# Two of the three split-precision products of 256-column activations under one pass of the weights

## The reference, cut to what matters

```python
def mixer_block(h, ...):                      # first block, 2 layers
    u = h @ w_in                              # 1024 x (proj + 4096 gate columns)
    ...
    g = jax.nn.sigmoid(gates.reshape(bsz, seq, N_BRANCH, D_MODEL))
    merged = (g[:, :, 0] * (y_a @ w_up_a) + g[:, :, 1] * (y_b @ w_up_b)
              + g[:, :, 2] * (y_c @ w_up_c) + g[:, :, 3] * (y_d @ w_up_d))
    return merged @ w_out

def swiglu(h, w_in, w_out):                   # w_in 1024 x 5632, w_out 2816 x 1024
    gate, up = jnp.split(h @ w_in, 2, axis=-1)
    return (jax.nn.silu(gate) * up) @ w_out
```

## Time and profile before

| | us |
|---|---|
| median of 3 runs | 2862.05 |
| profiled execution, its own time | 2864.3 |
| span of the profiled execution | 2862.5 |
| TensorE matmul busy | 2715.0 |
| TensorE weight loads busy | 2372.7 |
| VectorE busy | 1645.2 |
| ScalarE busy | 1133.2 |
| mean granted TensorE clock | 0.976 of 2.4 GHz |

### The profile page before, as it was taken

The page is one execution under the profiler, slowest core; times in us unless marked ns, Lnnn a source line. Parts: engine busy times, 40 slices in busy tenths (PEclk is TensorE's granted clock), DMA queues, the critical chain, the costliest instruction groups (busy, mean ns, idle before and its releaser), DMA issues.

```text
span 2862.5 us, 39149 instructions
## 1 busy us (share of the span) xinstructions
PE 2715.0 (95%) x16098; PEld 2372.7 (83%) x16098; DVE 1645.2 (57%) x2699; ACT 1133.2 (40%) x1743; POOL 0.3 (0%) x5
## 2 busy tenths in 40 slices
PE   7999899899989989999899989999989999899898
PEld 6999899899979978888664868888868888778898
DVE  6656777665567765555541555555555444655654
ACT  6464444545544442222232432222232222345443
POOL 0000000000000000000000000000000000000000
PEclk9999999999999989999999999999999999999999
DMA  5443577444347744444411024445434444311554
GB/s 187 170 139 112 169 228 225 158 148 148 111 169 226 224 154 155 148 137 153 143 53 66 30 74 132 141 146 153 149 103 146 141 154 144 128 38 45 177 175 135
DMA packets 114049, 403.22 MB, mean 141 GB/s; under 512 B 12368, under 2 KB 15568, under 8 KB 113744
## 3 DMA queue, kind: packets, MB, share of 16 engines
q1 hardware_dynamic: 113872, 400.72, 43.5%
HBM read 399.63 MB, written 1.05 MB: 140 GB/s over the span
## 4 chain that ended last, share of the span: by engine, by line
PE 91%; DVE 4%; ACT 3%; issue 2%; DMA 1%; SPq 0%; DVEq 0%; ACTq 0%
PE psum L533 26%; PE psum L534 25%; PE psum L535 25%; PE psum L829 2%; PE psum L856 1%; PE psum L956 1%; PE psum L964 1%; ACT whi L1034 1%; ACT L1062 1%; DVE wlo L1411 1%; PE psum L529 0%; PE psum L922 0%; PE psum L890 0%; PE psum L903 0%; PE psum L894 0%
## 5 line engine op out<-in xcount | busy, mean ns | idle before, releaser
L533 PE MATMUL psum<-HHI,whi 128*128 128x256 f32 (+1 forms) x3456 | 1126.4, 326 | 60.1 <-DVE HLO L1477 32.7
L534 PE MATMUL psum<-HLO,whi 128*128 128x256 f32 (+1 forms) x3456 | 1117.0, 323 | 0.0
L535 PE MATMUL psum<-HHI,wlo 128*128 128x256 f32 (+1 forms) x3456 | 1116.0, 323 | 0.0
L1411 DVE TENSOR_TENSOR wlo<-wring,whi 128x1024 fp32r<-128x1024 f32 x590 | 707.6, 1222 | 392.5 <-ACT whi L1034 390.0
L1034 ACT ACTIVATE whi<-wring 128x1024 fp32r<-128x1024 f32 x590 | 607.0, 1054 | 466.6 <-PE psum L535 442.8
L533 PEld LDWEIGHTS psum<-HHI,whi 128*128 128x128 f32 x3456 | 668.8, 194 | 126.6 <-issue 65.9
L534 PEld LDWEIGHTS psum<-HLO,whi 128*128 128x128 f32 x3456 | 669.1, 194 | 49.0 <-issue 1.4
L535 PEld LDWEIGHTS psum<-HHI,wlo 128*128 128x128 f32 x3456 | 668.4, 193 | 47.9
L533 PE MATMUL psum<-HIDHI,whi 128*128 128x256 f32 (+1 forms) x1056 | 357.2, 338 | 0.0
L534 PE MATMUL psum<-HIDLO,whi 128*128 128x256 f32 (+1 forms) x1056 | 357.2, 338 | 0.0
L535 PE MATMUL psum<-HIDHI,wlo 128*128 128x256 f32 (+1 forms) x1056 | 357.2, 338 | 0.0
(11 more groups left out here) (279 smaller groups left out, 2021.1 us busy)
## 6 DMA issues: line engine op xcount, KB each, us to landing
wring<-ffn_in SPq DMA_DIRECT2D x264, 512.0 KB, 4.2
wring<-mod_w SPq DMA_DIRECT2D x144, 512.0 KB, 4.3
wring<-ffn_out SPq DMA_DIRECT2D x96, 448.0 KB, 3.5
wring<-w_proj SPq DMA_DIRECT2D x66, 512.0 KB, 3.4
wring<-w_gate SPq DMA_DIRECT2D x64, 512.0 KB, 3.7
wring<-ffn_out SPq DMA_DIRECT2D x48, 512.0 KB, 4.0
wring<-w_up SPq DMA_DIRECT2D x20, 512.0 KB, 3.3
wring<-w_out SPq DMA_DIRECT2D x16, 512.0 KB, 3.5
```

The lines of the kernel that those rows point to most:

```text
L533: mm(out_, w[0], a[0], start=start, stop=False)
L534: mm(out_, w[0], a[1], start=False, stop=False)
L535: return mm(out_, w[1], a[0], start=False, stop=stop)
L1411: TTN(wlo[:, i, :], wring[:, raw_slot(tag, k), :], whi[:, i, :].bitcast(F32), ALU.subtract).then_inc(sem("weights_lo"), 1)
```

## The change

Where the moving side is 256 tokens wide, high and low activations are laid next to each other (`HPAIR[128, 8, 2, 256]`, `HIDPAIR[128, 22, 2, 256]`). The weights' high part then meets both in one matmul of 512 columns, and the weights' low part meets the high activations in a second one of 256 columns, which is added to the first half of the bank. So the bank ends with two sums, high x high + low x high in columns 0 to 255 and high x low in columns 256 to 511, and whoever reads it has to add them. This is done in `gate`, `wo`, in ffi and ffo of the first block, and in the last feed-forward. `proj`, the attentions and everything of 512 columns stay as they are.

The readers: of a gate lot, ScalarE copies the second half and VectorE adds the first. Of `wo` and `ffo`, VectorE adds both halves to X, one after the other, with a wait between. In `ffn` ScalarE copies up's second half to a new buffer `U1`, VectorE adds up's first half to it, the same for gate in `S`, then ScalarE's Silu works on the sum in SBUF, and VectorE multiplies. The order of these among the weights' high and low parts is changed, as the diff shows. The last feed-forward's norm now writes the packed places too.

```diff
+        HPAIR = sb("HPAIR", [P, KT, 2, SEQ], F32R, at=h_at)
+        HHI1, HLO1 = HPAIR[:, :, 0, :], HPAIR[:, :, 1, :]
...
+        HIDPAIR = sb("HIDPAIR", [P, FT, 2, SEQ], F32R, at=arena_at)
+        HIDHI1, HIDLO1 = HIDPAIR[:, :, 0, :], HIDPAIR[:, :, 1, :]
+        S1, U1 = (carve([("S", 2, SEQ)], 2 * FT * SEQ + a)["S"] for a in (0, 2 * SEQ))
...
         def first(tag):
-            return tag[0] in ("n1", "n2")
+            return tag[0] in ("n1", "n2") or tag == ("b2", 1)
...
+            def mm3_pair(bank, w, pair, start, stop):
+
+
+                mm(bank, w[0], pair, start=start, stop=False)
+                return mm(bank[:, 0:SEQ], w[1], pair[:, 0, :], start=False, stop=stop)
...
                 for k in GATE_LOTS[before]:
-                    dense_lot(f"gate{l}", k, SEQ, h_of(("n1", l)))
+                    dense_lot(f"gate{l}", k, SEQ, (HPAIR,))
...
-                dense(f"wo{l}", SEQ, h_of(("n1", l)), lambda c: done("merged", (l, c)))
+                dense(f"wo{l}", SEQ, (HPAIR,), lambda c: done("merged", (l, c)))
...
                 for j in range(FT):
                     k, slot = 2 * j + 1, j % 2
-                    act.wait_ge(*lot_done(tag_in, k))
-                    A(S_[:, slot, 0:n], bank_of((tag_in, k))[:, 0:n], ACT.Silu).then_inc(*freed((tag_in, k), "silu", (tag, j)))
-                    split_ahead(tag_in, k - 1)
+                    if n == SEQ:
+                        act.wait_ge(*lot_done(tag_in, k - 1))
+                        A(U1[:, slot, :], bank_of((tag_in, k - 1))[:, SEQ:BOTH], ACT.Copy).then_inc(*mark("up_lo", (tag, j)))
+                        split_ahead(tag_in, k - 1)
+                        act.wait_ge(*lot_done(tag_in, k))
+                        A(S_[:, slot, :], bank_of((tag_in, k))[:, SEQ:BOTH], ACT.Copy).then_inc(*mark("gate_lo", (tag, j)))
+                        act.wait_ge(*done("gate_sum", (tag, j)))
+                        A(S_[:, slot, 0:n], S_[:, slot, 0:n], ACT.Silu).then_inc(*mark("silu_done", (tag, j)))
...
                     split_ahead(tag_in, k)
                     act.wait_ge(*done("hid_t", (tag, j)))
                     A(hi[:, j, 0:n], S_[:, slot, 0:n], ACT.Copy).then_inc(*mark("hid_hi", (tag, j)))
...
-                    A(gate_places[k // 2][:, k % 2, :], bank_of((f"gate{l}", k))[:, 0:SEQ], ACT.Copy).then_inc(*freed((f"gate{l}", k), "logits", (l, k)))
+                    A(gate_places[k // 2][:, k % 2, :], bank_of((f"gate{l}", k))[:, SEQ:BOTH], ACT.Copy).then_inc(*mark("logits_lo", (l, k)))
...
                 for k in GATE_LOTS[before] if part is None else [GATE_LOTS[before][part]]:
+                    v.wait_ge(*done("logits_lo", (l, k)))
+                    bank = bank_of((f"gate{l}", k))
+                    place = gate_places[k // 2][:, k % 2, :]
+                    TTN(place, place, bank[:, 0:SEQ], ALU.add).then_inc(*freed((f"gate{l}", k), "logits", (l, k)))
                     if k + SLOTS < 4 * KT:
                         split_ahead(f"gate{l}", k)
...
+            def add_tile(m, bank, key, coef, n, event, l=0, pair=False):
+
+                if pair:
+                    x = X[:, m, 0:SEQ]
+                    a, b = bank[:, SEQ:BOTH], bank[:, 0:SEQ]
+                    if coef is None:
+                        ln(TTN(x, x, a, ALU.add))
+                        TTN(x, x, b, ALU.add).then_inc(*freed(key, "x_ready", event))
+                    else:
+                        c = MODS[:, l, coef * KT + m, 0:1]
+                        ln(STT(x, a, c, x, ALU.mult, ALU.add))
+                        STT(x, b, c, x, ALU.mult, ALU.add).then_inc(*freed(key, "x_ready", event))
+                    return
...
                 for j in range(FT):
                     k, slot, up = 2 * j + 1, j % 2, (tag_in, 2 * j)
-                    v.wait_ge(*done("silu", (tag, j)))
-                    TTN(S_[:, slot, 0:n], S_[:, slot, 0:n], bank_of(up)[:, 0:n], ALU.mult).then_inc(*freed(up, "hid_t", (tag, j)))
-                    split_ahead(tag_in, k - 1)
-                    split_ahead(tag_in, k)
+                    if n == SEQ:
+                        gate = bank_of((tag_in, k))
+                        v.wait_ge(*done("up_lo", (tag, j)))
+                        TTN(U1[:, slot, :], U1[:, slot, :], bank_of(up)[:, 0:SEQ], ALU.add).then_inc(*freed(up, "up_sum", (tag, j)))
+                        split_ahead(tag_in, k - 1)
+                        v.wait_ge(*done("gate_lo", (tag, j)))
+                        TTN(S_[:, slot, :], S_[:, slot, :], gate[:, 0:SEQ], ALU.add).then_inc(*freed((tag_in, k), "gate_sum", (tag, j)))
+                        split_ahead(tag_in, k)
+                        v.wait_ge(*done("silu_done", (tag, j)))
+                        TTN(S_[:, slot, :], S_[:, slot, :], U1[:, slot, :], ALU.mult).then_inc(*mark("hid_t", (tag, j)))
...
                     v.wait_ge(*done("hid_hi", (tag, j)))
                     TTN(lo[:, j, 0:n], S_[:, slot, 0:n], hi[:, j, 0:n].bitcast(F32), ALU.subtract).then_inc(*mark("hidden", (tag, j)))
```

More of the change, by code:

```diff
@@ L356, in first @@
         def first(tag):
-            return tag[0] in ("n1", "n2")
+            return tag[0] in ("n1", "n2") or tag == ("b2", 1)
         def h_of(tag):
-            return (HHI1, HLO1, T1) if first(tag) else (HHI, HLO, T2)
+            return (HHI1, HLO1, T1 if tag[0] != "b2" else T2) if first(tag) else (HHI, HLO, T2)
         def sq_of(tag):
-            return SQ1 if first(tag) else SQA if tag[0] == "b2" else SQ
+            return SQA if tag[0] == "b2" else SQ1 if first(tag) else SQ
         def hid_of(tag):
@@ L546, in open_wide @@
                         w = split_blocks(tag, j, KT, P)
-                        last = mm3(bank_of(key)[:, 0:n], (w[0][:, c, :], w[1][:, c, :]), (h[0][:, c, 0:n], h[1][:, c, 0:n]),
-                                   c == 0, c == KT - 1)
+                        wc = (w[0][:, c, :], w[1][:, c, :])
+                        if len(h) == 1:
+                            last = mm3_pair(bank_of(key), wc, h[0][:, c, :, :], c == 0, c == KT - 1)
+                        else:
+                            last = mm3(bank_of(key)[:, 0:n], wc, (h[0][:, c, 0:n], h[1][:, c, 0:n]), c == 0, c == KT - 1)
                         if c == KT - 1:
@@ L554, in tile3 @@
                 for c in range(KT):
-                    last = mm3(bank[:, 0:n], (w[0][:, c, :], w[1][:, c, :]), (h[0][:, c, 0:n], h[1][:, c, 0:n]), c == 0, c == KT - 1)
+                    wc = (w[0][:, c, :], w[1][:, c, :])
+                    if len(h) == 1:
+                        last = mm3_pair(bank, wc, h[0][:, c, :, :], c == 0, c == KT - 1)
+                    else:
+                        last = mm3(bank[:, 0:n], wc, (h[0][:, c, 0:n], h[1][:, c, 0:n]), c == 0, c == KT - 1)
                 return last
@@ L570, in dense, with operand @@
                     dense_lot(tag, k, n, h)
+            def operand(tag, n):
+                return (HPAIR,) if n == SEQ else h_of(tag)
             def ffn(tag_in, tag_out, tag, n):
-                dense(tag_in, n, h_of(tag), lambda c: done("h_ready", (tag, c)))
+                dense(tag_in, n, operand(tag, n), lambda c: done("h_ready", (tag, c)))
                 hi, lo, _ = hid_of(tag)
@@ L586, in ffn @@
                     for c in range(a, b):
-                        last = mm3(bank[:, 0:n], (w[0][:, c - a, :], w[1][:, c - a, :]), (hi[:, c, 0:n], lo[:, c, 0:n]),
-                                   c == 0, c == FT - 1)
+                        wc = (w[0][:, c - a, :], w[1][:, c - a, :])
+                        if n == SEQ:
+                            last = mm3_pair(bank, wc, HIDPAIR[:, c, :, :], c == 0, c == FT - 1)
+                        else:
+                            last = mm3(bank[:, 0:n], wc, (hi[:, c, 0:n], lo[:, c, 0:n]), c == 0, c == FT - 1)
                     lot_event(last, tag_out, k)
@@ L1068, in ffn @@
                     k, slot = 2 * j + 1, j % 2
-                    act.wait_ge(*lot_done(tag_in, k))
-                    A(S_[:, slot, 0:n], bank_of((tag_in, k))[:, 0:n], ACT.Silu).then_inc(*freed((tag_in, k), "silu", (tag, j)))
-                    split_ahead(tag_in, k - 1)
+                    if n == SEQ:
[6 more added lines that the diff above has]
+                        A(S_[:, slot, 0:n], S_[:, slot, 0:n], ACT.Silu).then_inc(*mark("silu_done", (tag, j)))
+                    else:
+                        act.wait_ge(*lot_done(tag_in, k))
+                        A(S_[:, slot, 0:n], bank_of((tag_in, k))[:, 0:n], ACT.Silu).then_inc(*freed((tag_in, k), "silu", (tag, j)))
+                        split_ahead(tag_in, k - 1)
                     split_ahead(tag_in, k)
```

18 lines of the change are left out of this document (10 added, 8 removed).

## The result

| | before | after |
|---|---|---|
| median of 4 runs each, us | 2862.46 (2861.99 to 2864.13) | 2964.14 (2962.53 to 2966.06) |
| span of the profiled execution | 2862.5 | 2962.1 |
| mean granted TensorE clock | 0.976 | 0.969 |

The ratio is 1.0355 [1.0341, 1.0368]: 3.5% slower. The forecast was 2951 in a range of 2925 to 2990. Between the two profiled executions the span grew by 99.6 us where the sum said 88.5.

A forecast was written before the change was run, and what follows sets the result against it. TensorE bounded the kernel before; after the change a ScalarE-VectorE hand-over chain would bound ffi. Chain +93.7, gate -2.3, wo -1.7, ffo -1.6 and last add +0.4 gave +88.5 on 2862.05: 2951 us, range 2925 to 2990.

The forecast's parts named there:

- the sum: Whole program: 93.7 - 2.3 - 1.7 - 1.6 + 0.4 = +88.5 us, added to a median of 2862.05.
- The chain: In ffi, ScalarE and VectorE hand-overs become the bound, 6.28 us a tile against TensorE's 5.53; +93.7 us, chance 0.85.
- The walk: One ffi tile followed through both queues from up copy to next up copy: 6.28 us, 8.57 with a modulation lot.
- the modulation lots: In ffi, each adds 2.29 us to a tile, 10 times in ffi0 and ffi1; three of 1.15 in the last.
- The small terms: Outside ffi: gate net -2.3 us, wo -1.7, ffo -1.6, the very last add to X +0.4.
- The paired step: On TensorE, 512 plus 256 columns replace three matmuls: 345.8 against 358.8 ns, 13.0 ns less a step.
- the 3.0 ns forecast: In ffo, a paired step takes 349.5 ns against 352.5, saving 3.0 ns over 528 steps.
- a dip in ffi: In ffi, a clock fall after a TensorE wait costs 1.7 us, fitting into 3.8 idle us of two tiles.
- The mixers' wait: In the gates, adds behind four low parts lengthen TensorE's wait, about 2.2 us per layer.
- TensorE as the bound: Rival: in ffi both other engines keep busy and TensorE still sets the pace, 2843 us; chance 0.08.
- Loads as the bound: Rival: weight loads set TensorE's pace, so a step falls to its columns' 320 ns, 2776 us; chance 0.02.
- Half clock throughout ffi: Rival: chain idling drops TensorE to 1.2 GHz throughout ffi, 10.2 us a tile, 3160 us; chance 0.05.

The follow-up runs named there:

- experiments on the order: Changed kernel with ffi's copies and sums moved ahead of high and low parts, product ahead of later low part and modulation lot: both 2851.28 us, singly 2877.39 and 2874.05.
- the kernel without the adds: Changed kernel with gate lots still paired, but ScalarE copying only the first half and VectorE's gate add left out: 2957.37 us, ratio 1.0334.
- another order: Changed kernel with both copies and sums first and product earlier in ffi: 2851.28 us; the same with gate and wo back at three matmuls: 2847.06 us.
- either half of the new order alone: Changed kernel with, in ffi, only the product moved ahead of the later low part and modulation lot: 2874.05 us; only both copies and sums first: 2877.39 us.
- The kernel with the better order: Changed kernel, same instructions, in ffi both copies and sums first and product ahead of the later low part and modulation lot: 2851.28 us, ratio 0.9963.
- another kernel: Changed kernel with only ffi's product moved ahead of the later low part and modulation lot, gates unchanged: 2874.05 us, ratio 1.0040.

## Why the prediction was right, and by how much it was off

**The chain was right in place and size.** Forecast were 161.6 us from the first up copy to the last HIDLO in layer 0 and 142.2 in the last feed-forward. The ends in the changed kernel:

```profile
345.14 0.39 ACT L1091 ACTIVATE arena<-psum 128x256 f32<-128x256 f32 x1 [5.73 <-PE psum L542]
...
506.18 0.43 DVE L1842 TENSOR_TENSOR HIDPAIR<-arena,HIDPAIR 128x256 fp32r<-128x256 f32 x1 [0.48 <-ACT HIDPAIR L1103]
...
2747.51 0.39 ACT L1091 ACTIVATE arena<-psum 128x256 f32<-128x256 f32 x1 [5.86 <-PE psum L542]
...
2889.31 0.43 DVE L1842 TENSOR_TENSOR HIDPAIR<-arena,HIDPAIR 128x256 fp32r<-128x256 f32 x1 [0.48 <-ACT HIDPAIR L1103]
```

506.61 - 345.14 = 161.5 and 2889.74 - 2747.51 = 142.2. The walk gave 6.28 and 8.57 us a tile; measured are 6.25 and 8.54. The walk worked because it followed both queues instruction by instruction and took the start of the next instruction, not the end of one, as what a piece costs. The experiments on the order show that this chain, and not the amount of work on any engine, is the cause. That the modulation lots add in full is shown too. The small terms beside it did worse, and nearly all their errors went one way, towards too low a time.

**The 11.1 us that the sum missed** lie outside it: 3.1 and 4.0 in the mixers, 5.3 in the three feed-forwards (1.8, 1.7 and 1.8), less 1.3 in stages that the change doesn't touch. The other 2 us between the forecast and the median come from the profiled execution of before, which took 2.2 us more than its median; that of after took what its median is (2963.89 us).

*The paired step was mis-sized.* The intervals were got by dividing stretches by counts, and the counts include matmuls cut by the edges; from start to start the same stretches of before have 120.0 and 226.7 ns in ffi, 118.3 and 233.3 in ffo. So a step of three was 360.0 ns, and the sum for a pair is 346.7, which leaves the saving at the forecast 13. In wo of layer 0 of the changed kernel, with no wait, the first matmul of a pair starts every 353 ns:

```profile
310.19 0.40 PE L541 MATMUL psum<-HPAIR,whi 128*128 128x512 f32 x1
...
310.54 0.40 PE L541 MATMUL psum<-HPAIR,whi 128*128 128x512 f32 x1
...
311.25 0.40 PE L541 MATMUL psum<-HPAIR,whi 128*128 128x512 f32 x1
```

So 7 ns are saved there, not 13.0. Over the whole mixers, gate and wo together, a step took 350.5 ns on average in layer 0 and 352.2 in layer 1, where it took 359.7 before: 9.2 and 7.5 saved. Over the 640 steps that is 3.0 us less than the sum has. In ffi it didn't matter, as TensorE waits there. In ffo a step went from 355.0 to 353 ns, so the 3.0 ns forecast became 2 or less, some 0.6 us over the 528 steps.

*The clock at the start of ffo was not priced.* The prediction saw that TensorE's idle time could bring the clock down, and argued that a dip in ffi is hidden. In ffi it is: the granted share of the stretch is 0.96 and the chain took its forecast time. But the last one falls where nothing hides it, after the wait for the last HIDLO:

```profile
506.76 0.52 PE L541 MATMUL psum<-HIDPAIR,whi 128*128 128x512 f32 x1 [3.53 <-DVE HIDPAIR L1842]
```

The next 3.5 us have a granted share of 0.56, near 1.2 GHz (the second stretch of the windows above), and that costs 3.5 x 0.44 = 1.5 us. The same stretch at the start of the other two ffo has 0.54 and 0.55. Three feed-forwards make 4.6 of the 5.3, and ffo's steps the rest. This was read from the traces, not tried by itself.

*The mixers' wait was priced, the clock behind it was not.* The 2.2 us for each layer stood for a later wait of TensorE. That one grew by 1.4, and two others by 0.5 to 0.7 together (at 158 us from 0.97 to 1.24, at 195 us from 0.40 to 0.81 in layer 0 and 0.60 in layer 1), so the price was about right, 0.5 too much in two layers. The fall of the clock behind it was missed, some 1.5 a layer in the profile taken. That gives 3.0 + 3.0 - 0.5 = 5.5 of the mixers' 7.1; the rest isn't found, and it is within the 2.4 us by which mixers of the same code differ from profile to profile. That the pairing alone does save there is shown by the step's 359.7 to 350.5 ns, and supported by the whole program: the kernel without the adds takes 2957.37 us, the one with three matmuls in gate and wo 2961.39.

**The rivals.** TensorE as the bound (2843) needed a chain under 5.53 us a tile, which the changed order doesn't give; with another order it came true at 2851 and 2847, so the mechanism was real and the order on the two queues decides it; either half of the new order alone gave back some 80% of the first feed-forward's loss. Loads as the bound are excluded by the same kernel (345 to 347 ns a step, not 320). Half clock throughout ffi: the granted share there is 0.96.

## What to carry to other kernels

Before an engine is relieved by splitting its result over two readers, walk one period of both readers' queues: two in-order engines that hand work to each other several times a period can set a pace that neither one's busy share shows (67% and 46% here). Put each piece that the other engine waits for ahead of pieces that only have to be ready later; here that order alone was worth 4%. Fewer, wider matmuls save only the surplus of each one that goes, here 2 to 13 ns, so this pays in stages of hundreds of steps whose readers have time in hand.

## What the runs showed of the hardware that was not expected

The paired step of 512 and 256 columns has two paces at full clock, with the same code and TensorE never waiting. The kernel with the better order, in ffi0:

```profile
399.94 0.39 PE L541 MATMUL psum<-HPAIR,whi 128*128 128x512 f32 x1
...
400.29 0.39 PE L541 MATMUL psum<-HPAIR,whi 128*128 128x512 f32 x1
...
400.98 0.39 PE L541 MATMUL psum<-HPAIR,whi 128*128 128x512 f32 x1
```

Here it is 347 ns (1.04 us for three steps), in the mixer of the changed kernel above 353 (1.06). Over whole stretches the two values stand apart clearly: the 22 tiles of this ffi run at 346.7 ns a step, which is the sum of the two intervals of before, and most ffo stages at 353.3. Within a stage one pace held until TensorE's next wait; after a wait it could be the other. From ffi to ffo it changed without a wait too, in this kernel at 461 us. As 353 ns had been assumed, the faster pace in three ffi, 1056 steps, makes 7.0 of the 9 us by which the kernel with the better order beat what was expected of it. What sets the pace was not tried and stays open.

A single wait can be followed by a fall of the clock, and need not be. After waits of 1.97, 2.16 and 3.53 us the granted share was 0.58, 0.53 and 0.56 over the next 3.5 to 4 us, which costs some 1.5 us beside the wait itself. But behind the same 1.97 us in another kernel it stayed at 1.00, as shown above, and in ffi0 of the changed kernel TensorE waits 2.46 us before 392.2 and 2.47 us before 407.0: the next 4 us have a share of 1.00 behind the first and 0.63 behind the second. So such a fall is a risk to be priced with a chance, not a fixed cost, and it moves a single profile by a us or two. What decides it was not tried.
